# Two column parts of the output projection taken tile by tile with the second norm and the router between them, and the shared gate and up products ahead of the routing counts

## The chip, the cores and the metric

The kernel runs on one core of one Trainium2 chip. The metric is the time of one execution on the device in microseconds (us), the median of several runs. The engines are TensorE (PE), VectorE (DVE), ScalarE (ACT), GpSimd (POOL) and SyncE (SP); SP, ACT and POOL also issue transfers, which the core's 16 DMA engines carry out.

## The reference

One layer of a hybrid decoder step: attention in three groups and a short convolution, one output projection, a second norm, then a mixture of 64 experts with 8 chosen per token. What matters here is the second half:

```python
x = x + g1 * (jnp.concatenate([attn, conv_out], axis=-1) @ w_o)          # 1024 x 1024
h2 = _rmsnorm(x, norm2_g) * (1 + sc2) + sh2
x = x + g2 * _moe(h2, w_router, b_router, ...)

def _moe(h, ...):
    scores = jax.nn.sigmoid(xt @ w_router)                                 # n x 64
    sel = scores + b_router          # top 2 of each group of 8 -> 4 groups -> top 8 experts
    w = w / jnp.sum(w, axis=-1, keepdims=True) * ROUTED_SCALE              # gates
    routed = sum over chosen experts of gate * (silu(x @ w_gate_e) * (x @ w_up_e)) @ w_down_e
    shared = (silu(xt @ w_gate_s) * (xt @ w_up_s)) @ w_down_s              # width 256
    return routed + shared
```

There are 544 tokens (512 of a prompt, 32 of a batch of decode samples), the model width is 1024, an expert's width is 256, and all is in float32.

## The kernel before, in words

The program is written out by hand, engine by engine; each engine runs its own list in the order written and waits on semaphores. Nothing reorders it. The tokens are five tiles in `ORDER`: first the 32 sample tokens (`SAMPLE`, j = 0), then four tiles of 128.

**Output projection.** `w_o` lies in three column parts of 384, 384 and 256 (`WO_W`). The loop runs over parts and inside each over the five tiles, so a unit u is 5 times the part plus the tile. PE computes a unit into bank `pb[u % 2]` (L1356; the sample tile's products, which use a quarter of the columns, at L1166) and may start unit u when the evacuation of unit u - 2 is over (`s_wg`). DVE multiplies the unit by the adaLN gate (L1799) and adds it to x (L1801); for the sample tile it first adds four quarters (L1626, L1628).

**Second norm and router.** When a tile's last part is added, ACT squares and sums its row (L1004), DVE makes mean and epsilon (L1768, `inverse_rms`), ACT takes the root (L1007), DVE inverts it (L1771) and makes the normed row in two instructions (L1784, L1786, `second_norm`); the second one signals `s_h2`. PE turns the row by eight transposes (L1089), ACT copies them to `h2T` (L1019), PE multiplies by the router's weights (L1368), and ACT takes the sigmoid (L1013). In the kernel before DVE does the norms of the first two tiles between the units of the last part, and those of the other three behind the projection; PE's turns and routers stand behind the whole projection.

**Routing.** From all scores DVE selects eight experts per token (L1822 to L1852), which gives the mask `r_mb` (`s_M`). PE counts the tokens of each expert and ranks them (`ranks`, L1396 to L1405), DVE sorts the 64 experts by count (L1873 to L1887, `s_pick`), PE forms the list of expert numbers (`served`, L1412), and DVE writes it to `meta` (L1891, `s_meta`). The gates are a chain of six DVE instructions (L1863 to L1868, `s_G`).

**Shared expert.** Gate and up are computed in two halves f = 0, 1 of the width: a product with `w_gate_s` and one with `w_up_s` for each (PE L1434 and L1437). ACT applies silu (L1031), DVE multiplies (`shared_mul`, L1859). `ranks` stands between the halves, and `served` between gate and up of the second. Then ten units of the down product (`shared_down`, L1453), with `places` (L1420, L1421) behind the first, and two `slots` (L1462) among them, which give the row numbers for the first gathers.

**Weights of the routed experts.** SP first writes the normed rows to DRAM (L591), waits for `s_G` and writes the gates (L594), waits for `s_meta`, reads four expert numbers into registers (L598), and then issues the loads of the first four experts (L602 gate and up, L606 down; 1 MB each, three per expert), the last two of them only after `shared_down`. In the loop of 16 passes, each with four experts, SP reloads a buffer when PE has used it: gate and up of the first two, down of the first two, gate and up of the last two, down of the last two. PE computes gate and up (L1497) and down (L1517); POOL gathers tokens (L766) and adds results to DRAM (L771).

## Time and profile before

| | us |
|---|---|
| median of 3 runs | 1240.82 (1238.19 to 1246.15) |
| the profiled execution, own time | 1241.44 |
| its span in the trace | 1239.6 |
| PE busy | 1088.4 (88%) |
| DVE busy | 436.6 (35%) |
| ACT busy | 210.9 (17%) |
| POOL busy | 257.0 (21%) |
| the chain that ended last, by engine | PE 50%, DMA 36%, DVE 6% |

The trace's times start at the span's start. A timeline row gives start, duration, engine, line of the program, operation, what it writes and reads, the count of instructions merged in it, and in brackets how long the engine had been idle before and what ended that. The chain is followed back from the last instruction: each piece is the work or the wait that the next one was waiting for. PEclk is TensorE's granted clock as a share of its full 2.4 GHz, so 0.5 is 1.2 GHz. The DMA share is the mean busy share of the 16 DMA engines.

### The profile page before, as it was taken

To read this page: it belongs to the slowest core of one execution; us is meant where nothing else is said; L and a number is where in the kernel's file an instruction comes from. 1 tells how busy PE (TensorE), PEld (TensorE's weight loads), DVE (VectorE), ACT (ScalarE), POOL (GpSimd) and SP (SyncE) were. 2 spreads that over 40 slices of the span, in tenths; PEclk is the share of its full clock that TensorE was granted. 3 is DMA by queue.
4 is the path that set the end of the run, shared out by engine and by line. 5 is a ranking of instruction groups with operands and counts; after the bars stand their busy time and mean duration, and the time that the engine had idled before them with its cause. 6 is when DMAs were issued, how large, how long until landed. Compare 5 with 4: busy or idle time off the path is not lost.

```text
span 1239.6 us, 16572 instructions
## 1 busy us (share of the span) xinstructions
PE 1088.4 (88%) x5866; PEld 537.3 (43%) x5866; DVE 436.6 (35%) x985; ACT 210.9 (17%) x455; POOL 257.0 (21%) x276
## 2 busy tenths in 40 slices
PE   6879999997998987989999999989988998899870
PEld 2445445554776565543333333333333333333330
DVE  1324776403456357132323213221322132213225
ACT  4311110002333013021111101110111011111110
POOL 1001223103121200012223122312221223122220
PEclk9989999996999998999999999999999999999995
DMA  9896789936562962197999999999999999999936
GB/s 318 327 345 218 227 287 320 232 127 212 168 190 94 348 239 90 70 411 266 388 384 374 371 381 390 387 370 368 386 388 350 373 376 386 364 358 382 375 88 233
DMA packets 80933, 370.73 MB, mean 299 GB/s; under 512 B 12913, under 2 KB 27358, under 8 KB 52695
## 3 DMA queue, kind: packets, MB, share of 16 engines
q1 hardware_dynamic: 47088, 258.50, 52.3%
q0 software_dynamic: 26176, 79.62, 23.9%
q10 hardware_dynamic: 7636, 32.17, 7.2%
q8 instruction: 21, 0.34, 0.1%
q14 instruction: 12, 0.10, 0.0%
HBM read 342.62 MB, written 66.02 MB: 330 GB/s over the span
## 4 chain that ended last, share of the span: by engine, by line
PE 50%; DMA 36%; DVE 6%; issue 3%; SPq 2%; ACT 1%; POOL 1%; ACTq 0%; DVEq 0%; POOLq 0%
DMA mem<-in_w_up_e 31%; PE pb L1497 14%; PE pb L1201 8%; PE pb L1356 4%; PE pb L1205 3%; PE pb L1517 3%; DMA new_d<-mem 2%; PE pb L1089 2%; PE pb L1116 2%; PE pb L1434 2%; PE pb L1334 2%; PE pb L1288 1%; SPq L602 1%; PE pb L1275 1%; DMA mem<-in_w_ada 1%
## 5 line engine op out<-in xcount | busy, mean ns | idle before, releaser
L1497 PE MATMUL pb<-mem 128*32 128x512 f32 (+2 forms) x1792 | 349.2, 603 | 26.1 <-DMA mem<-in_w_up_e 25.8
L1497 PEld LDWEIGHTS pb<-mem 128*32 128x32 f32 (+2 forms) x1792 | 119.2, 130 | 242.3 <-issue 241.8
L1517 PE MATMUL pb<-mem 128*32 128x512 f32 (+2 forms) x896 | 177.5, 597 | 2.6 <-issue 2.6
L1089 PE MATMUL pb<-mem 128*128 128x128 f32 (+2 forms) x649 | 95.1, 283 | 61.1 <-ACT mem L1046 27.4
L1987 DVE SCALAR_TENSOR_TENSOR mem<-pb,mem 128x256 f32<-128x256 f32 x48 | 32.5, 676 | 319.2 <-ACT mem L1059 250.9
L771 POOL DMA_INDIRECT y_d<-mem x48 | 69.7, 1453 | 302.0 <-DVE mem L1993 160.7
L1201 PE MATMUL pb<-mem 128*128 128x384 f32 x384 | 131.3, 497 | 0.0
L1089 PEld LDWEIGHTS pb<-mem 128*128 128x128 f32 (+2 forms) x649 | 72.6, 146 | 119.4 <-issue 48.4
L1517 PEld LDWEIGHTS pb<-mem 128*32 128x32 f32 (+2 forms) x896 | 57.0, 129 | 97.8 <-issue 97.8
L766 POOL DMA_INDIRECT mem<-h_d,mem x54 | 60.8, 1126 | 179.6 <-issue 135.3
L1201 PEld LDWEIGHTS pb<-mem 128*128 128x128 f32 x384 | 72.5, 193 | 58.2 <-issue 9.6
L1059 ACT ACTIVATE mem<-pb 128x256 f32<-128x256 f32 x48 | 18.4, 383 | 344.2 <-PE pb L1497 344.2
L1993 DVE COPY mem<-pb 128x512 f32<-128x512 f32 x48 | 33.2, 691 | 103.0 <-PE pb L1517 103.0
L1356 PE MATMUL pb<-mem 128*128 128x384 f32 (+1 forms) x192 | 55.9, 452 | 0.0
L771 POOL DMA_INDIRECT z_d<-mem x32 | 45.8, 1432 | 36.7 <-DVE mem L1993 27.8
L1356 PEld LDWEIGHTS pb<-mem 128*128 128x128 f32 x192 | 36.2, 190 | 19.7 <-issue 1.2
L694 POOL DMA_DIRECT2D mem<-in_cache_k_w x24 | 12.8, 535 | 153.7 <-DVE mem L1620 96.7
L1930 DVE TENSOR_TENSOR mem<-mem 128x320 bf16<-128x320 f32 (+3 forms) x90 | 43.8, 551 | 2.0 <-DMA y_d<-mem 2.0
L1958 DVE COPY mem<-pb 128x512 f32<-128x512 f32 x51 | 35.3, 692 | 23.5 <-PE pb L1089 23.2
L1205 PE MATMUL pb<-mem 128*128 128x512 f32 x96 | 42.7, 597 | 0.0
L1068 ACT ACTIVATE mem<-pb 128x512 f32<-128x512 f32 x48 | 28.6, 595 | 76.9 <-PE pb L1517 76.9
L1046 ACT ACTIVATE mem<-pb 128x512 f32<-128x512 f32 x51 | 30.5, 597 | 48.2 <-PE pb L1089 48.2
(261 smaller groups left out, 984.1 us busy)
## 6 DMA issues: line engine op xcount, KB each, us to landing
mem<-in_w_gate_e SPq DMA_DIRECT2D x64, 1024.0 KB, 15.4
mem<-in_w_up_e SPq DMA_DIRECT2D x64, 1024.0 KB, 24.2
mem<-in_w_down_e SPq DMA_DIRECT2D x64, 1024.0 KB, 22.8
mem<-in_w_ada SPq DMA_DIRECT2D x24, 1024.0 KB, 10.0
mem<-in_w_in SPq DMA_DIRECT2D x8, 1536.0 KB, 14.1
mem<-new_d POOLq DMA_DIRECT2D x16, 512.0 KB, 6.9
out<-in_cache_k_w ACTq DMA_DIRECT2D x8, 1020.0 KB, 14.9
out<-in_cache_v_w ACTq DMA_DIRECT2D x8, 1020.0 KB, 20.3
```

The lines of the kernel that those rows point to most:

```text
L766: eng.indirect_dma_start(out=xg[t][:], out_offset=None, in_=h2_d, in_offset=bass.IndirectOffsetOnAxis(ap=ix[:, t:t + 1], axis=0), bounds_c ...
L771: eng.indirect_dma_start(out=to, out_offset=bass.IndirectOffsetOnAxis(ap=ixs[0:hi - lo, col:col + 1], axis=0), in_=yo[t][lo:hi, :], in_off ...
L1089: return eng.transpose(dst, src, ident[0:parts, 0:parts])
L1201: mm = eng.matmul(pb[z % 2][0:nt(tt), 0:PJ_W], lhsT=hT[:, k, tok(tt)], rhs=w[:, k, :], start=(k == 0), stop=(k == KD - 1))
L1205: eng.matmul(pb[z % 2][:, :], lhsT=w[:, k, P * j:P * (j + 1)], rhs=hT[:, k, 0:SEQ], start=(k == 0), stop=(k == KD - 1))
L1356: mm = eng.matmul(pb[u % 2][0:nt(tt), 0:WO_W[o]], lhsT=catT[:, k, tok(tt)], rhs=w[:, k, :], start=(k == 0), stop=(k == KD - 1))
L1497: mm = eng.matmul(pb[t % 2][lo:hi, :].rearrange("p (q f) -> p q f", q=2), lhsT=xT[t][:, k, lo:hi], rhs=wgu[c][:, :, k, :], start=(k == 0), ...
L1517: mm = eng.matmul(pb[2 + half][lo:hi, :], lhsT=he[t][:, f, lo:hi], rhs=wdn[c][:, f, 512 * half:512 * half + 512], start=(f == 0), stop=(f ...
L1930: last = eng.tensor_tensor(oneh[:, :, lo:lo + n], pos[:, :, at_].to_broadcast([P, TILES, n]), const("place")[:, p0:p0 + n].unsqueeze(1).to ...
L1958: eng.tensor_copy(xT[t][:, 4:8, :], pb[5][:, :].rearrange("p (k n) -> p k n", k=4)).then_inc(s_xd, 1)
L1987: eng.scalar_tensor_tensor(out=hh[t].rearrange("p (k f) -> p f k", k=2), in0=pairs(pb[t % 2][:, FE:2 * FE]), scalar=gcol[t], in1=pairs(sge ...
L1993: eng.tensor_copy(yo[t][:, 512:D], pb[3][:, :]).then_inc(s_yd, 1)
```

## The change

The projection's parts 1 and 2 are taken tile by tile (`WO_UNITS`): part 0 over all tiles as before, then for each tile its unit of part 1 and its unit of part 2. The norm of tile j - 1 is split on DVE around the second unit of tile j, and PE's turn of tile j - 1 and router of tile j - 2 follow PE's two units of tile j (`NORMED`). Four small DVE instructions that prepare routing tables move from the end of the projection to between part 0 and part 1. ACT's work takes the same order. Both halves of the shared gate and up stand ahead of `ranks`; the rest of the routing follows, then `places`, and then `shared_down` without a break but for `slots`, two units earlier than before. DVE's `shared_mul(0)` moves ahead of the mask and the gates' chain behind `shared_mul(1)`. `w_up_s` gets a buffer of its own (slot 10) and is loaded behind `w_gate_s`; SP issues the load of `w_down_s` ahead of the last normed row.

```diff
+WO_UNITS = [(0, j) for j in range(TILES)] + [(o, j) for j in range(TILES) for o in (1, 2)]
 def wo_done(u):
-    return u + 1 + 3 * (u // 5 + 1)
+    return u + 1 + 3 * sum(ORDER[j] == SAMPLE for _, j in WO_UNITS[:u + 1])
+NORMED = ((), (0,), (1,), (2,), (3, 4))
...
-    slots += [0, 1, 2, 0, 1, 2]
+    slots += [0, 1, 2, 0, 10, 2]
...
         ring += [at(m, ADA_W) for m in (m_mod, m_mod + ADA_W, m_qk + NVEC * VL, m_qk + NVEC * VL + ADA_W, m_cv,
-                                        m_vr + 512, m_att)]
+                                        m_vr + 512, m_att, m_mod + HROW)]
...
+                kind, i = items[n]
+                if kind == "sup":
+                    eng.wait_ge(s_add, 16)
+                    eng.wait_ge(s_fold, len(WIDE))
...
-                        eng.wait_ge(s_wo, wo_done(5 * i0 + 4))
+                        eng.wait_ge(s_wo, wo_done(WO_UNITS.index((i0, TILES - 1))))
...
+            last = ring_uses("sdown", 0)
+            for n in range(last):
+                ring_load(n)
             for j, tt in enumerate(ORDER):
+                if j == TILES - 1:
+                    ring_load(last)
                 eng.wait_ge(s_h2, j + 1)
                 eng.dma_start(h2_d[tok(tt), 0:D], h2_row[j % 2][0:nt(tt), :]).then_inc(s_h2w[j % 2], 16)
             eng.wait_ge(s_G, 1)
...
             eng.wait_ge(s_scb, 16 * ZW)
+            eng.wait_ge(s_su, 4)
             load_dn(1, first[1])
-            eng.wait_ge(s_su, 4)
...
+            for j in range(TILES):
+                squares(j)
+                for i in NORMED[j]:
+                    turned(i)
+                    if i:
+                        if i == 1:
+                            eng.wait_ge(s_rz, 1)
+                        sigmoid(i - 1)
             sigmoid(TILES - 1)
             for f in range(2):
-                if f:
-                    eng.wait_ge(s_route, 2)
-                    eng.activation(rT[:, 0:512], pb[0][0:NE, :], ACT.Copy)
-                    eng.activation(rT[:, 512:TILES * P], pb[1][0:NE, 0:P], ACT.Copy).then_inc(s_rT, 1)
                 eng.wait_ge(s_su, 2 * f + 1)
                 eng.activation(sg[:, f, 0:SEQ], pb[4 * f][:, :], ACT.Silu)
                 eng.activation(sg[:, f, SEQ:NTOK], pb[4 * f + 2][:, 0:NS], ACT.Silu).then_inc(s_sg, 1)
+            eng.wait_ge(s_route, 2)
+            eng.activation(rT[:, 0:512], pb[0][0:NE, :], ACT.Copy)
+            eng.activation(rT[:, 512:TILES * P], pb[1][0:NE, 0:P], ACT.Copy).then_inc(s_rT, 1)
...
+            for u in range(TILES):
+                project(u)
+            for j in range(TILES):
+                project(TILES + 2 * j)
+                project(TILES + 2 * j + 1)
+                for i in NORMED[j]:
+                    second_turn(i)
+                    if i:
+                        router(i - 1)
             router(TILES - 1)
...
             for f in range(2):
                 if f:
-                    ranks()
                     eng.wait_ge(s_sc, TILES)
                 for q, n in ((0, n_g), (1, n_u)):
-                    if f and q:
-                        eng.wait_ge(s_pick, 1)
-                        served(0, NE)
                     w = ring[slots_of[n]][:, 0:KD * FE].rearrange("p (k n) -> p k n", k=KD)
                     for k in range(KD):
                         eng.matmul(pb[4 * f + q][:, :], lhsT=w[:, k, P * f:P * (f + 1)], rhs=h2T[:, k, 0:SEQ],
                         mm = eng.matmul(pb[4 * f + q + 2][:, 0:NS], lhsT=w[:, k, P * f:P * (f + 1)],
                                         rhs=h2T[:, k, SEQ:NTOK], start=(k == 0), stop=(k == KD - 1))
                     mm.then_inc(s_su, 1)
+            ranks()
+            eng.wait_ge(s_pick, 1)
+            served(0, NE)
             eng.wait_ge(s_pick, 2)
             eng.matmul(pb[2][0:NE, 0:1], lhsT=upper[0:NE, 0:NE], rhs=e_units, start=True, stop=True)
             eng.matmul(pb[2][0:1, 1:2], lhsT=ones[0:NE, 0:1], rhs=e_units, start=True, stop=True
                        ).then_inc(s_route, 1)
             ring_in(n_d)
             wd = ring[slots_of[n_d]][:, 0:2 * D].rearrange("p (k n) -> p k n", k=2)
-            eng.wait_ge(s_hs, 2)
             def shared_down(u):
...
+            eng.wait_ge(s_pick, 3)
+            served(NE, P)
+            eng.wait_ge(s_sg, 2)
+            places()
+            eng.wait_ge(s_hs, 2)
             for u in range(10):
                 shared_down(u)
-                if u == 0:
-                    eng.wait_ge(s_pick, 3)
-                    served(NE, P)
-                    places()
-                if u == 5:
+                if u == 3:
                     slots(0)
-                if u == 8:
+                if u == 6:
                     eng.wait_ge(s_ix, 1)
                     slots(1)
             eng.wait_ge(s_ysh, 10)
...
+            def gated_sum(u):
...
+                eng.wait_ge(s_wo, wo_done(u))
...
+                    whole = part[:, 0:w]
+                eng.tensor_tensor(wt[u % 2][0:n, 0:w], whole, m2[s][0][0:n, c0:c0 + w], ALU.mult).then_inc(s_wg, 1)
+                eng.wait_ge(s_wg, u + 1)
+                eng.tensor_tensor(x_t[0:n, tt, c0:c0 + w], x_t[0:n, tt, c0:c0 + w], wt[u % 2][0:n, 0:w], ALU.add
+                                  ).then_inc(s_x1, 1)
+            for u in range(TILES):
+                gated_sum(u)
             eng.wait_ge(s_vout, 16 * (DIL * G + 1))
             link(eng.memset(r_mb, 0.0))
...
-            for j in range(2, TILES):
-                inverse_rms(j)
-            for j in range(2, TILES):
-                second_norm(j)
+            for j in range(TILES):
+                gated_sum(TILES + 2 * j)
+                if j:
+                    inverse_rms(j - 1)
+                gated_sum(TILES + 2 * j + 1)
+                if j:
+                    second_norm(j - 1)
+            inverse_rms(TILES - 1)
+            second_norm(TILES - 1)
             link(eng.tensor_copy(slotb[:, 0:15], const("slot")[:, 0:15]))
...
-            link(eng.reciprocal(r_den, r_den))
-            link(eng.tensor_scalar(r_den, r_den, 2.5, None, ALU.mult))
-            eng.tensor_tensor(r3(r_g), r3(r_g), r_den.unsqueeze(2).to_broadcast([P, TILES, NE]), ALU.mult
-                              ).then_inc(s_G, 1)
+            eng.tensor_tensor(r_mb[:, 0:SAMPLE * NE], r_ma[:, 0:SAMPLE * NE], r_mr[:, 0:SAMPLE * NE], ALU.not_equal
+                              ).then_inc(s_M, 1)
+            eng.tensor_tensor(r_mb[0:NS, SAMPLE * NE:RW], r_ma[0:NS, SAMPLE * NE:RW], r_mr[0:NS, SAMPLE * NE:RW],
+                              ALU.not_equal).then_inc(s_M, 1)
...
             link(eng.tensor_reduce(e_iters[0:1, :], e_small[0:1, :], AX, ALU.add))
             link(eng.tensor_scalar(meta[0:1, P:P + 1], e_iters[0:1, :], float(QUART), None, ALU.add))
             shared_mul(1)
+            link(eng.tensor_tensor(r_g, r_sc, r_mb, ALU.mult))
+            link(eng.tensor_reduce(r_den, r3(r_g), AX, ALU.add))
+            link(eng.tensor_scalar(r_den, r_den, 1e-30, None, ALU.max))
+            link(eng.reciprocal(r_den, r_den))
+            link(eng.tensor_scalar(r_den, r_den, 2.5, None, ALU.mult))
+            eng.tensor_tensor(r3(r_g), r3(r_g), r_den.unsqueeze(2).to_broadcast([P, TILES, NE]), ALU.mult
+                              ).then_inc(s_G, 1)
```

Place 1, PE in parts 1 and 2. Before, behind part 2 (L1356 is the projection, L1089 the turn of a normed row, L1368 the router; 128x256 is a unit of part 2):

```order
L1356 MATMUL pb<-mem 128x256 [waits s_wg]
L1356 MATMUL pb<-mem 128x256 x7
L1356 MATMUL pb<-mem 128x256 [waits s_wg]
L1356 MATMUL pb<-mem 128x256 x7
L1089 MATMUL pb<-mem 128x32 [waits s_h2,s_wr]
L1089 MATMUL pb<-mem 128x32 x7
L1089 MATMUL pb<-mem 128x128 [waits s_h2T,s_h2]
L1089 MATMUL pb<-mem 128x128 x3
L1089 MATMUL pb<-mem 128x128 [waits s_h2T]
L1089 MATMUL pb<-mem 128x128 x3
L1368 MATMUL pb<-mem 32x64 [waits s_h2T]
L1368 MATMUL pb<-mem 32x64 x7
```

Of the change, the units of tile 1, the turn of tile 0, the units of tile 2 and the turn of tile 1 (L1382 is the projection, L1114 the turn):

```order
L1382 MATMUL pb<-mem 128x384 [waits s_wg,s_ring1]
L1382 MATMUL pb<-mem 128x384 x7
L1382 MATMUL pb<-mem 128x256 [waits s_wg,s_ring2]
L1382 MATMUL pb<-mem 128x256 x7
L1114 MATMUL pb<-mem 128x32 [waits s_h2]
L1114 MATMUL pb<-mem 128x32 x7
L1382 MATMUL pb<-mem 128x384 [waits s_wg,s_ring1]
L1382 MATMUL pb<-mem 128x384 x7
L1382 MATMUL pb<-mem 128x256 [waits s_wg,s_ring2]
L1382 MATMUL pb<-mem 128x256 x7
L1114 MATMUL pb<-mem 128x128 [waits s_h2T,s_h2]
L1114 MATMUL pb<-mem 128x128 x3
```

The turn of the tile before, with its wait for `s_h2`, now stands directly behind a tile's unit of part 2, and the next tile's unit of part 1 stands behind the turn.

DVE at the same place of the change (L1834 and L1836 evacuate a unit, L1802 and L1805 are `inverse_rms`, L1818 and L1820 `second_norm`, the last of which signals `s_h2`; tile 1, norm of tile 0):

```order
L1834 TENSOR_TENSOR mem<-pb,mem 128x384 [waits s_wo]
L1836 TENSOR_TENSOR mem<-mem 128x384 [waits s_wg]
L1802 TENSOR_SCALAR mem<-mem 32x1 [waits s_ss2]
L1805 RECIPROCAL mem<-mem 32x1 [waits s_sd2]
L1834 TENSOR_TENSOR mem<-pb,mem 128x256 [waits s_wo,s_m2,s_link]
L1836 TENSOR_TENSOR mem<-mem 128x256 [waits s_wg]
L1818 SCALAR_TENSOR_TENSOR mem<-mem 32x1024
L1820 TENSOR_TENSOR mem<-mem 32x1024 [waits s_link]
```

The norm of tile 0, which stood among the evacuations of part 2, now follows the evacuation of tile 1's unit of part 2, which waits for PE by `s_wo`.

Place 2, DVE behind the tokens' selection. Before (L1859 and L1860 are `shared_mul(0)`, L1863 to L1868 the gates' chain, then the sorting of experts):

```order
L1859 TENSOR_TENSOR mem<-pb,mem 128x512 [waits s_sg,s_su,s_M]
L1860 TENSOR_TENSOR mem<-pb,mem 128x32
L1863 TENSOR_TENSOR mem<-mem 128x320
L1864 TENSOR_REDUCE mem<-mem 128x5 [waits s_link]
L1865 TENSOR_SCALAR mem<-mem 128x5 [waits s_link]
L1866 RECIPROCAL mem<-mem 128x5 [waits s_link]
L1867 TENSOR_SCALAR mem<-mem 128x5 [waits s_link]
L1868 TENSOR_TENSOR mem<-mem 128x320 [waits s_link]
L1873 SCALAR_TENSOR_TENSOR mem<-pb,mem 64x64 [waits s_route]
L1875 SCALAR_TENSOR_TENSOR mem<-pb,mem 64x1
```

Of the change, ten rows behind the expert numbers' copy to `meta` (L1940 is the last of the iterations' count, L1893 and L1894 are `shared_mul(1)`, L1942 to L1947 the gates' chain):

```order
L1940 TENSOR_SCALAR mem<-mem 1x1 [waits s_link]
L1893 TENSOR_TENSOR mem<-pb,mem 128x512 [waits s_sg,s_su,s_link]
L1894 TENSOR_TENSOR mem<-pb,mem 128x32
L1942 TENSOR_TENSOR mem<-mem 128x320
L1943 TENSOR_REDUCE mem<-mem 128x5 [waits s_link]
L1944 TENSOR_SCALAR mem<-mem 128x5 [waits s_link]
L1945 RECIPROCAL mem<-mem 128x5 [waits s_link]
L1946 TENSOR_SCALAR mem<-mem 128x5 [waits s_link]
L1947 TENSOR_TENSOR mem<-mem 128x320 [waits s_link]
```

The chain of the gates moved from ahead of the sorting to behind `shared_mul(1)`, so that `s_G` now comes later than `s_meta`.

SP at the same place of the change (L612 writes the gates, L616 reads the expert numbers into registers; the first load, L620, stands behind four such readings):

```order
L612 DMA h_d<-mem 128x64 [waits s_G]
L612 DMA h_d<-mem 128x64 x3
L612 DMA h_d<-mem 32x64
L616 TENSOR_LOAD mem [waits s_meta]
L616 ISA x2
```

SP's order here did not move: the gates' rows with their wait for `s_G` stand ahead of the wait for `s_meta` and of the first load.

Place 3, PE at the shared gate and up. Before (L1434, L1437 the products, L1396 to L1405 `ranks`, L1412 `served`):

```order
L1434 MATMUL pb<-mem 128x512 x8
L1437 MATMUL pb<-mem 128x32 x8
L1396 MATMUL pb<-mem 64x64 [waits s_hs,s_M]
L1396 MATMUL pb<-mem 64x64 x4
L1399 MATMUL pb<-mem 64x1 x5
L1405 MATMUL pb<-mem 64x128 x15
L1434 MATMUL pb<-mem 128x512 [waits s_sc]
L1434 MATMUL pb<-mem 128x512 x7
L1437 MATMUL pb<-mem 128x32 x8
L1412 MATMUL pb<-mem 1x64 [waits s_pick]
L1434 MATMUL pb<-mem 128x512 x8
```

Of the change (L1465, L1468 the products, L1431 to L1440 `ranks`, L1447 `served`):

```order
L1465 MATMUL pb<-mem 128x512 [waits s_sc]
L1465 MATMUL pb<-mem 128x512 x7
L1468 MATMUL pb<-mem 128x32 x8
L1465 MATMUL pb<-mem 128x512 x8
L1468 MATMUL pb<-mem 128x32 x8
L1431 MATMUL pb<-mem 64x64 [waits s_hs,s_M]
L1431 MATMUL pb<-mem 64x64 x4
L1434 MATMUL pb<-mem 64x1 x5
L1440 MATMUL pb<-mem 64x128 x15
L1447 MATMUL pb<-mem 1x64 [waits s_pick]
```

`ranks` stood behind the first half; it now stands behind both, and `served` follows it at once.

## Rows read from the trace of the kernel before

**Rows 1.** Chain that ended last, in order of time: start, duration, piece of work.

```profile
486.79 6.92 PE pb L1434 x16
493.71 1.71 PE pb L1437 x16
...
558.49 10.68 PE pb L1497 x48
...
596.75 10.63 PE pb L1497 x48
...
665.59 29.83 DMA mem<-in_w_up_e
...
695.65 7.10 PE pb L1497 x32
...
736.87 8.80 PE pb L1497 x32
```

**Rows 2.** Windows: stretch and length; PEclk, DMA share, GB/s.

```profile
520.00:560.00 40.00, 0.96 0.96 392
560.00:576.00 16.00, 1.00 0.50 161
576.00:665.00 89.00, 1.00 1.03 378
665.00:1148.00 483.00, 0.99 1.01 376
```

**Rows 3.** Timeline of SP's issues: start, duration, row.

```profile
507.07 2.22 SPq L594 DMA_DIRECT2D h_d<-mem  x5
520.32 0.36 SPq L602 DMA_DIRECT2D mem<-in_w_gate_e  x1
```

**Rows 4.** Timeline of PE, projection to shared down: start, duration, row, idle ahead.

```profile
424.43 20.91 PE L1356 MATMUL pb<-mem 128*128 128x384 f32 x64
...
446.27 14.08 PE L1356 MATMUL pb<-mem 128*128 128x256 f32 x64
...
470.06 1.94 PE L1089 MATMUL pb<-mem 128*128 128x128 f32 x8 [9.11 <-ACT mem L1019]
...
482.18 1.10 PE L1089 MATMUL pb<-mem 128*128 128x128 f32 x8 [1.23 <-DVE mem L1786]
...
528.83 2.98 PE L1453 MATMUL pb<-mem 128*32 128x512 f32 x4 [2.74 <-DVE mem L1860]
```

**Rows 5.** Timeline of DVE, evacuations and norms in the projection.

```profile
424.64 0.55 DVE L1626 COPY mem<-pb 32x384 f32<-32x384 f32 x1 [0.38 <-PE pb L1166]
...
426.99 0.55 DVE L1799 TENSOR_TENSOR mem<-mem 32x384 f32<-32x384 f32 x1
...
454.87 2.07 DVE L1784 SCALAR_TENSOR_TENSOR mem<-mem 32x1024 f32<-32x1024 f32 x1
...
458.91 0.41 DVE L1799 TENSOR_TENSOR mem<-pb,mem 128x256 f32<-128x256 f32 x1
```

**Rows 6.** Timeline of PE in the input projection.

```profile
155.91 0.37 PE L1089 MATMUL pb<-mem 32*128 32x32 f32 x3 [1.90 <-DVE mem L1665]
...
157.20 7.12 PE L1201 MATMUL pb<-mem 128*128 128x384 f32 x16
```

**Rows 7.** Window of PE: stretch, length, busy; PEclk, DMA share, GB/s.

```profile
464.00:475.00 11.00, 4.74 (x29) 0.53 0.41 150
```

**Rows 8.** Timeline of DVE, gates' chain to the expert numbers.

```profile
504.87 0.48 DVE L1863 TENSOR_TENSOR mem<-mem 128x320 f32<-128x320 f32 x1
...
506.96 0.21 DVE L1873 SCALAR_TENSOR_TENSOR mem<-pb,mem 64x64 f32<-64x64 f32 x1
...
508.84 0.15 DVE L1887 TENSOR_REDUCE mem<-mem 64x1 f32<-64x8 f32 x1
517.04 0.22 DVE L1891 CAST mem<-pb 1x64 int32<-1x64 f32 x1 [8.05 <-PE pb L1412]
526.13 0.23 DVE L1898 TENSOR_SCALAR mem<-mem,pb 1x16 f32<-1x16 f32 x1 [8.87 <-PE pb L1442]
```

## What the change is expected to do

> **What bounds the kernel now.** I read the chain of waits first, since it says which engine the end hangs on at each time. It runs on PE from the shared gate product at 486.8 to the first pass of the expert loop at 558.5, and on in passes of 38.2 us (558.49 to 596.75); from 665.6 it goes over to the landing of expert weights, and PE's product for the last two experts then starts every 41.2 us (695.65 to 736.87) [rows 1]. So one sees PE first and transfers later. The chain does not say how much room the transfers had before 665. The windows do: from 576 to 1148 the DMA engines are full (share 1.03 and 1.01, 378 and 376 GB/s); from 520 to 560 they are as good as full too (0.96, with the start in it); only from 560 to 576 is the share 0.50, that is 16 x 0.50 = 8.0 us of idle transfer time [rows 2]. SP issues the first expert load at 520.3 [rows 3]. The amount of data from there on is fixed. So from the first load to the end of the loop the kernel has 8.0 us of slack in its transfers, and a first load that comes later by more than that moves the end, unless PE holds it back more. Two quantities are needed: how much later (or earlier) the first load is issued, and how much PE's loop start moves. The time of the first load is made up of S, the start of the shared gate product (486.8 before), and what lies between S and the load.
>
> **The projection, before S.** Before, the projection ends at 446.27 + 14.08 = 460.3, PE then sits idle 9.1 us for DVE's norms, and S follows at 486.8, 26.5 us after the projection's end [rows 1, 4]. The change takes routers and turns under the projection, but a wait goes with them. On PE the turn of tile j - 1 stands directly behind tile j's unit of part 2; on DVE the norm of tile j - 1 stands behind the evacuation of that same unit. The norm therefore cannot start until PE has finished the unit, and PE has nothing to do but wait for it. The wait is an evacuation, two instructions of about 0.42 or 0.9 us with gaps, and a norm, 454.87 to 458.91 or 4.1 us [rows 5], with 0.1 for signals: 5.1 us. Queued behind the waiting turn are the router and the next tile's two units; ACT's copies and SP's row writes come after it in any case. It happens for tiles 1, 2 and 3 within the projection: 3 x 5.1 = 15.3 us.
>
> The sample tile costs too. DVE now has four small instructions ahead of its evacuation in part 1. The nearest row, one over 320 columns, takes 0.48 [rows 8], so they are between nothing and 1.9 us; two of them are on half as many columns and less, and I take 1.1. Before, DVE began the evacuation at 424.6 after 0.4 us of idle and its multiply ended at 426.99 + 0.55 = 427.5 [rows 5]; it is now 0.7 later, 428.3. PE needs only 1.1 us more for the sample tile's unit of part 2 from 424.4, to 425.5, and its next unit wants that bank: 2.8 us of idle PE.
>
> Turns and routers moved ahead: a turn is 1.1 us, and two routers take the 3.5 us from 483.28 to 486.79 [rows 1, 4]. Turns of tiles 0 to 2 (0.7 + 1.1 + 1.1) and routers of 0 and 1 (3.5) add 6.5 us to the projection's end: 460.3 + 2.8 + 15.3 + 6.5 = 484.9. Behind it stand an evacuation 0.9, norm of tile 3 4.1, `inverse_rms` 0.6 and norm of tile 4 4.1, under which PE's turn and router of earlier tiles are hidden, and then the same 4.6 us as before from the last turn to S (482.18 to 486.79): 14.3 us. S at full clock is 499.2, which is 12.4 us later than before. The 26.5 us behind the projection do shrink to 14.3; the waits inside cost more than that gives. The extra changes of ACT's function tables (four more) stand in ACT's waiting times; without that cover each lies ahead of a root or a sigmoid. I take nothing for them.
>
> **The clock.** What PE did before the clock fell: the 9.1 us of idle ahead of 470.06 [rows 4] are followed by the stretch 464 to 475 with a granted clock of 0.53, the lower level, 1.2 GHz [rows 7], and there a turn takes 1.94 where it takes 1.10 at full clock. After only 1.90 us idle and a short turn, a unit of 128x384 takes 7.12 us [rows 6], where the projection takes 20.91 / 4 = 5.2 [rows 4]: 1.9 us lost. The turn at 482.18, behind 1.23 us of idle, shows no such loss. The waits of the change are 2.8 and three of 5.1 before S, each ahead of units of that kind, so the bounds are 0 (none falls) and 4 x 1.9 = 7.6 (all fall); they lie nearer to the rows that lose, and I take 7.6. The fourth wait of 5.1 is behind the projection, where PE waits for the last norm anyway, and costs nothing. S comes to 506.8, 20.0 us later.
>
> The Trainium skill, page "TensorE: Matmul & The Clock Gate", section "HAM oscillation — how this bites in real kernels", describes just this pattern: a wait that returns with every tile drops the clock anew each time, so that every tile starts at the half rate and the cost is paid per tile. By that rule the term is 7.6; by the row of 482.18 alone, where a short idle cost nothing, it would be 0. The two losing rows of this trace agree with the rule.
>
> **From S to the first load.** A gate or up product is 6.92 + 1.71 = 8.63 us [rows 1]. Four of them now precede `ranks`, 34.5 us. From the start of `ranks`: 0.5 us until DVE has the counts, its sorting 2.0 (506.96 to 508.99), 0.5 for PE's two small products, 2.6 for the next DVE stretch with `shared_mul(1)` (526.13 to 528.7, where PE resumes [rows 4]), and then the gates' chain 2.1 (504.87 to 506.96): `s_G` at 7.7 [rows 8]. `s_meta` is ready earlier, but SP's queue has the gates' rows first: 2.2 us of issuing [rows 3], and then the reading of four expert numbers, 520.32 - 517.26 = 3.1 us [rows 3, 8]. This reading was not behind `s_G` before; the gates' rows had been written at 507 to 509, 8 us ahead of `s_meta`. The first load is at S + 34.5 + 7.7 + 2.2 + 3.1 = S + 47.5, against S + 33.5 before: 14.0 us more. Loads start 20.0 + 14.0 = 34.0 us later, at 554.3.
>
> **The sum.** Less the 8.0 us of slack the end is 26.0 us later, if the idle of 560 to 576 goes away fully. It does if the second pass's loads are issued before the first twelve have landed: those kept the engines full for some 40 us before, so now until about 595; PE's loop start moves to about 574 (next), and it frees the first buffers 14.8 us later, at 589. PE itself moves less: from S to the loop was 71.7 us [rows 1], and of that the 2.7 us of idle ahead of `shared_down` [rows 4] and a clock loss behind it of 1.9 or so go away, as both halves are then done: 20.0 - 4.6 = 15.4 us later. So transfers decide. Own time of the profiled execution 1241.4 + 26.0 = 1267.4; it stands 0.6 above the median of 1240.8, so 1267. The earlier `slots`, the buffer for `w_up_s` (loaded behind `w_gate_s`, used 60 us later) and the later issue of `w_down_s` move neither quantity.
>
> **Rivals.**
> - PE decides: the late loads are caught up in the passes, which PE takes at 38.2 and transfers at 41.2. For it speaks that the chain is on PE until 665; against it the full share from 576 on. The end moves with PE, 15.4 us: 1256.
> - The clock stays up in all waits: 26.0 - 7.6 = 18.4 later, 1259. Against it rows 6 and 7. Together with the first rival: 20.0 - 7.6 - 4.6 = 7.8, or 1249, within 1% of before.
> - The norms are hidden, as the change's words say: PE's turn finds its row ready. The 15.3 and three of the four clock losses (5.7) go: 26.0 - 21.0 = 5.0, or 1246. Against it the order of both engines, in which nothing can move.
> - Faster or no slower, by one mechanism: the transfers' pass gets shorter, because loads meet gathers and scatters at another phase. While weights alone move, the rate would allow it: PE's own pass is 38.2. Over 15 passes the loss of 26.0 is made up when a pass falls by 1.7 us, to 39.5; at 38.4 the kernel would be at 1241.4 + 26 - 42, 1225. Against it: 378 GB/s in 576 to 665 and 376 after it, though the phase differs.
>
> **Chances and range.** The forecast has 0.75, PE decides 0.07, full clock 0.07, both together 0.04, hidden norms 0.03, shorter passes 0.04. The likeliest's own range is 1259 (no clock loss) to 1275 (each clock loss 2.5 us, and SP's reading or the norms' signals 1 us each dearer). The range to all but 2 in 10 is 1252 to 1275. A measurement can tell about 1% from no change, 12 us. Faster by over 1%: 0.03; within 1%, 1228 to 1253: 0.07; slower 0.90.
>
> **What the profile would show.** Four idle stretches of PE of about 5.1 us ahead of the turns in the projection, put down to DVE's second norm instruction, and one of 2.8 after the sample tile; PEclk at half behind them; S near 507; the gates' rows issued near 549 and the first expert load near 554, behind `s_meta` by over 5 us; no window of share 0.5 between the first load and 600; the chain on transfers from the second pass on instead of the fourth. I am wrong if PE turns without waiting, if the share falls below 1 after the first load, or if passes differ from 41.2 us.

## The result, and the profile after

The changed kernel takes 1263.65 us (median of 4 executions, 1262.48 to 1268.09) against 1239.72 for the kernel before on the same chip (4 executions): ratio 1.0181, 95% interval 1.0137 to 1.0225. It is slower, by 23.9 us; forecast were 26.

In the fourteen traces the output projection begins at 394.95 to 400.74 us, ahead of the first changed instruction that matters, while kernels with the same order from there on agree within 1 us in the distances behind it. So I compare distances: from the projection's start (call it P) to S (start of the shared gate product), from S to L (first pass of the expert loop), from L to the end of the span. P is this row, of the kernel before and then of the changed kernel (start, duration, row, idle ahead):

```profile
400.74 1.50 PE L1166 MATMUL pb<-mem 128*32 128x384 f32 x16 [0.81 <-issue]
```

```profile
394.95 1.50 PE L1191 MATMUL pb<-mem 128*32 128x384 f32 x16 [0.81 <-issue]
```

The chain of waits of the changed kernel, which answers to [rows 1]:

```profile
502.89 6.92 PE pb L1465 x16
509.81 1.71 PE pb L1468 x16
...
556.19 0.37 PE pb L1495 x15
...
561.13 17.05 DMA mem<-h_d,mem
...
578.31 1.94 PE pb L1114 x8
580.25 11.20 PE pb L1531 x48
...
619.04 10.63 PE pb L1531 x48
...
679.25 7.04 PE pb L1531 x32
...
687.87 29.66 DMA mem<-in_w_up_e
```

| | before | after | change | forecast |
|---|---|---|---|---|
| P to S | 486.79 - 400.74 = 86.1 | 502.89 - 394.95 = 107.9 | +21.9 | +20.0 |
| S to L | 558.49 - 486.79 = 71.7 | 580.25 - 502.89 = 77.4 | +5.7 | -4.6 |
| L to the end | 1239.6 - 558.49 = 681.1 | 1260.6 - 580.25 = 680.4 | -0.8 | +10.6 |
| P to the end | 838.9 | 865.7 | +26.8 | +26.0 |

(The medians differ by 23.9: that these two traces give 26.8, and their bare spans 21.0, is the scatter of P and of single executions.) The first row and the sum are about as forecast; the second and third are both wrong, and cancel. In the chain one sees what is new: ahead of the loop PE hangs on a gather of 17.05 us, the third of three (before it was the first one, and 7.39 us, see below; of the three, the slowest took 8.2 us before), and behind the loop's start the chain stays on PE for 106 us (580.25 to 686.3), nearly as before (107, 558.49 to 665.6), then goes over to transfers. It does not go over at the second pass.

The timeline of PE in the projection, where [rows 4] showed one wait of 9.11 us:

```profile
422.46 8.85 PE L1382 MATMUL pb<-mem 128*128 128x384 f32 x32 [2.88 <-DVE mem L1834]
436.37 1.05 PE L1114 MATMUL pb<-mem 32*128 32x32 f32 x8 [5.06 <-DVE mem L1820]
437.36 11.02 PE L1382 MATMUL pb<-mem 128*128 128x384 f32 x32
453.81 1.97 PE L1114 MATMUL pb<-mem 128*128 128x128 f32 x8 [5.43 <-DVE mem L1820]
455.70 1.91 PE L1404 MATMUL pb<-mem 128*32 128x64 f32 x16
457.55 9.47 PE L1382 MATMUL pb<-mem 128*128 128x384 f32 x32
472.08 1.68 PE L1114 MATMUL pb<-mem 128*128 128x128 f32 x8 [5.06 <-DVE mem L1820]
473.56 3.52 PE L1404 MATMUL pb<-mem 128*128 128x64 f32 x16
476.86 10.02 PE L1382 MATMUL pb<-mem 128*128 128x384 f32 x32
491.94 1.97 PE L1114 MATMUL pb<-mem 128*128 128x128 f32 x8 [5.05 <-DVE mem L1820]
```

L1820 is the norm's second instruction on DVE. The waits are those of the forecast: 2.8 (2.88) and four of 5.1 (5.06, 5.43, 5.06, 5.05). Behind each of the four the clock is down (granted 0.50, 0.50, 0.55 and 0.50 in 437 to 441, 454 to 458, 472 to 476 and 492 to 497): a unit of 8.85 us takes 11.02, 9.47, 10.02, a turn of 1.09 takes up to 1.97. Behind the wait of 2.88 it is not (1.00 in 422 to 431).

The windows, which answer to [rows 2]: stretch, length, busy times, then PEclk, DMA share and GB/s at the end of the row.

```profile
422.00:503.00 81.00, 59.95 (x249) 46.00 (x250) 32.48 (x45) 20.20 (x36) 0.56 (x1) 0.81 0.40 155
572.00:580.00 8.00, 5.51 (x24) 4.77 (x25) 1.84 (x5) 1.75 (x3) 0.00 (x0) 0.50 1.02 423
580.00:1148.00 568.00, 519.40 (x2990) 207.49 (x2989) 148.86 (x403) 80.87 (x169) 149.22 (x116) 0.99 1.01 376
592.00:600.00 8.00, 8.00 (x50) 2.68 (x46) 1.53 (x5) 1.50 (x4) 0.00 (x0) 1.00 0.75 299
```

From 572 to 580, where PE turns the gathered rows at half clock, the transfers are full. The gap behind the first loads is still there, at 592 to 600: 8 x 0.25 = 2.0 us idle, of the 8.0 before. SP's timeline answers to [rows 3]:

```profile
545.19 2.22 SPq L612 DMA_DIRECT2D h_d<-mem  x5
550.53 0.36 SPq L620 DMA_DIRECT2D mem<-in_w_gate_e  x1
551.56 0.33 SPq L620 DMA_DIRECT2D mem<-in_w_gate_e  x1
...
553.92 0.33 SPq L620 DMA_DIRECT2D mem<-in_w_gate_e  x1
```

The first load stands at S + 47.6 (550.53 - 502.89); forecast was S + 47.5. Last, ACT's timeline, where it evacuates the shared rows (L1064) and sends them to memory (`y_d`):

```profile
559.41 1.31 ACT L1064 ACTIVATE mem<-pb 128x512 f32<-128x512 f32 x2 [2.58 <-DMA y_d<-mem]
...
565.95 1.09 ACT L1064 ACTIVATE mem<-pb 128x512 f32<-128x512 f32 x2 [5.23 <-DMA y_d<-mem]
...
570.78 1.08 ACT L1064 ACTIVATE mem<-pb 128x512 f32<-128x512 f32 x2 [3.74 <-DMA y_d<-mem]
```

ACT sits 11.6 us idle for the writes of earlier rows (8.2 before), since there are two row buffers, and PE's turn at the end of this waits 4.50 us for ACT. Rows' writes and gathers are both issued while expert weights are in flight: the third gather is issued 10.6 us behind the first load (561.13 - 550.53), where it was 28.4 us before (548.75 - 520.32). The same place in the chain of the kernel before:

```profile
543.82 0.37 PE pb L1462 x15
...
545.82 7.39 DMA mem<-h_d,mem
```

### The profile page after: what moved, and what is told of

It is laid out like the page before. It is cut to its first block, busy times and chain, and to the rows that moved or that the text cites. A ratio compares the mean times of both kernels' runs of the same rounds, so it can differ in the third digit from the quotient of the medians.

```text
span 1260.6 us, 16592 instructions
## 1 busy us (share of the span) xinstructions
PE 1098.2 (87%) x5866; PEld 545.0 (43%) x5866; DVE 435.8 (35%) x985; ACT 216.2 (17%) x459; POOL 256.7 (20%) x276
## 4 chain that ended last, share of the span: by engine, by line
PE 54%; DMA 33%; DVE 6%; issue 2%; ACT 1%; SPq 1%; POOL 1%; ACTq 0%; DVEq 0%; POOLq 0%
DMA mem<-in_w_up_e 28%; PE pb L1531 15%; PE pb L1226 8%; PE pb L1382 5%; PE pb L1551 4%; PE pb L1230 3%; PE pb L1114 3%; PE pb L1465 2%; DMA new_d<-mem 2%; PE pb L1141 2%; PE pb L1359 2%; DMA mem<-h_d,mem 1%; PE pb L1313 1%; SPq L620 1%; PE pb L1300 1%
## 5 line engine op out<-in xcount | busy, mean ns | idle before, releaser
L1114 PE MATMUL pb<-mem 128*128 128x128 f32 (+2 forms) x649 | 99.4, 292 | 75.4 <-ACT mem L1071 25.7
L1114 PEld LDWEIGHTS pb<-mem 128*128 128x128 f32 (+2 forms) x649 | 76.5, 152 | 133.5 <-issue 42.1
L1084 ACT ACTIVATE mem<-pb 128x256 f32<-128x256 f32 x48 | 18.4, 383 | 344.8 <-PE pb L1531 344.8
L1382 PE MATMUL pb<-mem 128*128 128x384 f32 (+1 forms) x192 | 60.3, 475 | 2.9 <-DVE mem L1834 2.9
L789 POOL DMA_INDIRECT z_d<-mem x32 | 45.9, 1433 | 36.4 <-DVE mem L2032 27.6
L1382 PEld LDWEIGHTS pb<-mem 128*128 128x128 f32 x192 | 38.2, 202 | 24.2 <-issue 7.7
```

The source lines that it names most:

```text
L789: eng.indirect_dma_start(out=to, out_offset=bass.IndirectOffsetOnAxis(ap=ixs[0:hi - lo, col:col + 1], axis=0), in_=yo[t][lo:hi, :], in_off ...
L1114: return eng.transpose(dst, src, ident[0:parts, 0:parts])
L1382: mm = eng.matmul(pb[u % 2][0:nt(tt), 0:WO_W[o]], lhsT=catT[:, k, tok(tt)], rhs=w[:, k, :], start=(k == 0), stop=(k == KD - 1))
```

## The experiments

Two theories. **A:** the end follows L at a fixed 681 us, and L is late by the projection and by small transfers that stand behind weights. **B:** the end follows the first expert load, less the slack. B is the prediction's rule without its clause "unless PE holds it back more"; with the clause the rule is the later of the two, and it gives A wherever the loads still have room. The first four experiments split the change and its two halves.

**Only the projection.** The change's projection and turns, the routing of before: `shared_gate_up` of the second half behind the counts, the gates' chain ahead of sorting.

> The projection of the change (tile by tile, own buffer for w_up_s) with the routing order of before. Shared gate starts 18 to 19 us later than before, the first expert load the same 18 to 19 us later. Theory A (PE's loop start decides): the way from there to the loop is 71.7 us as before, so the loop and the end are 18 to 19 us later, near 1258 to 1259. Theory B (transfers decide, 8.0 us of slack): 18.5 - 8 = 10.5 us later, 1250 to 1251.

**Only the routing.** The reverse: the projection of before, and the change's order from S on.

> The projection of the kernel before (all units, then the turns and routers as before) with the change's order of the routing. Both theories put the start of the shared gate product at 486-488 us, the first expert load at 527-530 (8-10 later than before, by the gates' chain that now stands behind sorting) and the idle share of the DMA engines ahead of 600 us larger than before. Theory A (the end follows the start of PE's expert loop): from S to the loop 76-78 us, as in the changed kernel, so a loop start at 563-565 and a time of 1245-1247 (4-6 over before). Theory B (the part from the gate product on costs only what the first load's delay leaves over the slack in the transfers): 8-10 us fit in the 8 us of slack, 1241-1243.

**Turn one tile later,** on PE, all else as changed:

```diff
             for j in range(TILES):
                 project(TILES + 2 * j)
+                if j >= 2:
+                    second_turn(j - 2)
+                    if j > 2:
+                        router(j - 3)
                 project(TILES + 2 * j + 1)
-                for i in NORMED[j]:
-                    second_turn(i)
-                    if i:
-                        router(i - 1)
+            second_turn(3)
+            router(2)
+            second_turn(4)
+            router(3)
             router(TILES - 1)
```

> The change, but PE's turn of tile j - 1 and the router behind it stand behind the first unit of tile j + 1 instead of directly behind the second unit of tile j. Both theories: the waits of 5.1 us inside the projection go (15.3 us) and three losses of clock with them (5 to 6 us); shared gate starts near 483 instead of 503. The end falls by about 20 us to 1243 to 1245, still a few us above before (1240), because the routing order of the change is kept. If it stays above 1255, the waits on the norm were not what cost.

**Turn one tile later, routing of before.**

> The projection tile by tile with the turn one unit later (as in e2_turn_later) and the routing order of before. Shared gate starts 3 to 5 us earlier than before, and the rest is as before: theory A (the end follows PE's loop start) gives 1235 to 1237 against 1240 before; theory B gives the same or, where transfers decide, the same 3 to 5 us, since loads and loop move together.

The medians, the ratios to the kernel before on the same chip with intervals (its median is 1239.72 to 1242.25 by chip), and the distances, all read on PE's timeline (which puts S and L up to 0.2 us off the chain of waits above):

| projection, routing | median, us | ratio | P to S | S to L | L to end |
|---|---|---|---|---|---|
| before, before | 1239.72 | 1 | 85.9 | 71.9 | 681.1 |
| before, changed | 1246.82 | 1.0037 [1.0014, 1.0061] | 85.9 | 78.4 | 680.7 |
| changed, before | 1262.6 | 1.016 [1.0097, 1.0223] | 107.8 | 73.6 | 681.2 |
| changed, changed | 1263.65 | 1.0181 [1.0137, 1.0225] | 107.8 | 77.3 | 680.5 |
| later, changed | 1245.72 | 1.0022 [0.9995, 1.0049] | 84.0 | 77.3 | 681.2 |
| later, before | 1236.62 | 0.995 [0.9925, 0.9976] | 84.1 | 70.7 | 680.1 |

In these traces the first load stands 29.5 to 41.5 us ahead of L, and the last column does not move with it. In the run with the projection alone the first load was only 18.3 us later than before (538.57 against 520.32 [rows 3]), the loop 21.6: the end came 21.7 later in the span (1261.3 against 1239.6). That is A; by B it would have been 18.3 - 8.0 = 10.3, and by the prediction's rule with its clause 21.6, like A. A's own figure, 1258 to 1259, was missed by 4 us, as the loop moved 21.6 and not 18 to 19. The place of the turn is all of the projection's cost: 107.8 becomes 84.0, below the 85.9 of before. In the trace with the later turn only the last of the four waits of 5.1 us is left (5.06 us at 469.19), beside the 2.88. And the routing costs time with two of the projections: S to L is 78.4 or 77.3 where the old order has 71.9 or 70.7. With the changed projection it is 77.3 against 73.6, and the ratios, 1.0181 and 1.016, do not tell the two apart; part of the 73.6 is a lower clock ahead of the gathers (20 instructions of `shared_down` in 10.65 us instead of 8.97).

**Gates' chain first.** The changed kernel with the gates' block on DVE (L1942 to L1947) ahead of sorting again, so that only the first load moves.

> The changed kernel with the gates' chain on DVE (five operations and the product) put back ahead of the sorting. Both theories: the gates' rows go out and the first expert load is issued 4-6 us earlier (545-546 instead of 550.5). Theory A (the end follows the loop start, which waits for the gathers and the shared rows' writes): the loop start does not come earlier, 579-583, since the ranks, and with them the gathers, come some 3-5 us later and stand behind the loads; time 1262-1266. Theory B (the first load's place decides, as the prediction had it): 5 us less, 1257-1259.

1267.56 us, 1.0197 [1.0153, 1.0241]. SP's and then PE's timeline:

```profile
548.37 0.36 SPq L620 DMA_DIRECT2D mem<-in_w_gate_e  x1
```

```profile
507.82 7.09 PE L1465 MATMUL pb<-mem 128*128 128x512 f32 x16
...
585.10 11.42 PE L1531 MATMUL pb<-mem 128*128 128x512 f32 x48
```

The first load is at S + 40.6 instead of S + 47.8 on this timeline, 7.2 us earlier; L is at S + 77.3 and the end at L + 680.7, both as in the changed kernel. B is out: 7.2 us of the first load's place are worth nothing here. The prediction's rule with its clause is not, since an earlier load cannot bring the end ahead of PE's.

**Gathers ahead of the third expert's loads.** In SP's program:

```diff
             load_dn(1, first[1])
+            for t in range(ET):
+                eng.wait_ge(s_ga[t], 16)
             load_gu(2, first[2])
```

> The change, but SP waits for the first three gathers to have landed before it issues the loads of the third and fourth expert. Theory A (the end follows PE's loop start, and in the change that start is late because the first gathers, 17.1 us to landing, and the shared expert's row writes stand behind 10 MB of expert weights): the gathers land some 8 us earlier, near 568 to 570 us, the loop starts 5 to 8 us earlier than the change's 580.3, and the kernel takes 1256 to 1259 us. Theory B (the end follows the amount of transfer from the first load on, as predicted): the transfers of the third and fourth expert start later, so the kernel takes the change's 1264 us or up to 6 us more.

1269.47, 1.0195 [1.0143, 1.0248]. L at S + 76.6: a miss. ACT's writes held PE as before (4.56 us), and from L to the end it was 684.4, 3.9 us longer. The third gather took 15.8 us.

**A third row buffer,** so that ACT need not wait for the writes of tiles 0 and 1: `y_row[j % 3]` with a semaphore of its own, in memory where SP loads the fourth expert's gate and up only later.

> The changed kernel with a third buffer for the rows of the shared expert, so that ACT's evacuation of tiles 2 and 3 no longer waits for the write of tile 0 and 1 to memory (2.58 + 5.23 + 3.74 = 11.6 us of waits in the trace of after, and PE's 4.50 us ahead of the turns of the first expert behind it). If that wait is what sets the loop's start: PE's 4.5 us go, less what the third gather (landing at 578.2) then holds: loop start 575.5-578 instead of 580, time 1259-1262. If the gathers decide alone: 579-580 and 1263.

1267.07, 1.0198 [1.0155, 1.0242]; L at S + 77.2, as the expectation's second case has it, but slower than its 1263. PE's timeline ahead of the loop shows what took the wait's place:

```profile
572.55 1.07 PE L1115 MATMUL pb<-mem 128*128 128x128 f32 x8 [1.00 <-DMA mem<-h_d,mem]
577.35 1.94 PE L1115 MATMUL pb<-mem 128*128 128x128 f32 x8 [3.73 <-DMA mem<-h_d,mem]
582.38 1.94 PE L1115 MATMUL pb<-mem 128*128 128x128 f32 x8 [3.09 <-DMA mem<-h_d,mem]
```

No turn waits for ACT any more (4.50 us in the changed kernel), but the three turns wait 7.8 us for the three gathers, issued at 562.33, 563.96 and 565.27.

**Both together.**

> The changed kernel with both causes taken away at once: the third buffer for the shared rows, and SP issues the loads of the third expert only when the three gathers of the first have landed. One of the two alone left the start of the expert loop at S + 76.6 and S + 77.2 us (S: start of the shared gate product), since the other took its place. If the rows' writes and the gathers behind the bulk loads are the whole of what the part from S to the loop is longer than forecast, the loop now starts at S + 72 to 74, 3-5 us earlier than in the changed kernel, and the time is 1259-1262, if the loads held back do not come back later (in the run with the gathers ahead alone, 3.9 us were lost from the loop's start to the end, 684.4 instead of 680.5). If it is something else (the ranks, POOL's three issues), S + 77 again.

1269.59, 1.0223 [1.018, 1.0266], a miss: L at S + 76.6, the third gather still 16.29 us, from L to the end 684.9. So holding the third expert's loads does not relieve the gathers: 6 MB of the first two experts' weights are issued ahead of them in any case (10 MB in the changed kernel).

**Gathers ahead of all but the first 2 MB.** The same three waits of SP, but behind `load_gu(0, ...)`, in the kernel with two row buffers.

> The changed kernel, with SP holding all expert loads but the first expert's gate and up (2 of the 6 MB that stand ahead of the gathers in the changed kernel) until the three gathers have landed. If the gathers take 17 us because these megabytes stand before them: 7-9 us each instead of 10-17, third landing at S + 66-68 instead of S + 75.4, the rows' writes faster too, and the loop starts at S + 68-70 instead of 77.3. The price is what the held loads cost later: they start some 13 us later than in the changed kernel. If the end follows the loop's start alone, 8 us earlier, 1255-1257; if the transfers decide once they are this late, the loop's gain is given back: 1262-1268. If the gathers stay at 17 us, the loads are not their cause.

1271.0, 1.0235 [1.0195, 1.0275]. The chain of waits of this run:

```profile
566.26 6.91 DMA mem<-h_d,mem
...
578.21 30.42 DMA mem<-in_w_up_e
...
608.86 9.67 PE pb L1533 x32
```

The gather takes 6.91 us instead of 17.05, ACT waits at most 2.30 us for a write instead of 5.23, and L is at S + 70.7 (578.55 - 507.86), 6.6 us earlier. The cause of the late loop is thereby shown: weights ahead of the small transfers. The chain also shows the price. The weights held back land at 608.6 and PE waits 8.27 us in its first pass; from L to the end it is 690.5, 10 us more, and the time is above the 1262 to 1268 expected. So the slack of the loads does end.

**Where it ends.** The transfers of all fourteen traces say it. SP's first reload of a used buffer comes 14.8 to 16.1 us behind L. Windows from about L + 4 to L + 20 of the changed kernel, then gates' chain first, gathers ahead of the third expert, gathers ahead of all but 2 MB:

```profile
584.00:600.00 16.00, 16.00 (x94) 5.35 (x96) 4.45 (x11) 2.02 (x5) 4.86 (x7) 1.00 0.88 360
589.00:605.00 16.00, 16.00 (x94) 5.42 (x96) 4.46 (x11) 2.02 (x5) 4.90 (x7) 1.00 0.55 188
588.80:604.80 16.00, 16.00 (x94) 5.42 (x96) 4.09 (x11) 2.02 (x5) 4.78 (x7) 1.00 1.01 403
582.50:598.50 16.00, 16.00 (x100) 5.36 (x102) 3.96 (x11) 2.02 (x5) 4.37 (x7) 1.00 1.02 418
```

The changed kernel still has 16 x 0.12 = 1.9 us of idle transfers there, gates' chain first has 7.2 (its loads are 7.2 us earlier), the kernel before 6.9. In the eleven traces with an end at L + 680.1 to 681.2 the idle time is 1.4 to 8.3 us; in the three with a later end (684.4, 684.9, 690.5) there is none. From L + 20 on all fourteen move 376 or 377 GB/s. So the transfers do set the pace of the rest, and the idle share is the room of the first loads, but counted from L: while some of it is left, the stream that decides begins with the reloads, which PE releases, and the end follows L. Up to L + 20 the eleven have moved 18.8 to 19.3 MB (in the changed kernel 49.5 us at 384 GB/s), the run with all but 2 MB held 15.2: the missing 3.8 MB are 10.1 us at 377 GB/s, and the end is 10.0 us later. For the other two, 18.3 and 18.1 MB, this gives about 2 us of the 3.9 and 4.4.

**Matmuls in the waits.** Work that nothing reads is added ahead of the turns:

```diff
+                if j <= 3:
+                    for k in range(5 if j else 3):
+                        eng.matmul(pb[6][:, :], lhsT=catT[:, k % KD, tok(0)], rhs=catT[:, k % KD, 0:SEQ],
+                                   start=(k == 0), stop=(k == (4 if j else 2)))
                 for i in NORMED[j]:
                     second_turn(i)
```

> The changed kernel with matmuls of 512 columns that nothing reads, put ahead of the turns in the first four tiles of the output projection (3, then 5 in each of three), where PE waits for the norm: added work, for the clock's sake. If the clock losses behind the waits are a cost of the change (prediction: 4 of 1.9 us; the trace of after: three units of 11.02, 9.47 and 10.02 us where 8.85 is the full-clock one), the granted clock stays at 1.0 through the projection, the three units take 8.85, the shared gate product starts at 497-499 instead of 502.7, and the end comes 4-6 us earlier than the changed kernel's: 1257-1260. If the losses come from something else than the idle time, or the added matmuls take longer than the waits they fill (5 x 0.22 = 1.1 of 5.1 us each at full clock, so there is room), the time stays at 1263 or rises.

1264.34, 1.0168 [1.0123, 1.0213], a miss of the 1257 to 1260 expected: the time cannot be told from the changed kernel's. PE's timeline:

```profile
436.28 4.45 PE L1415 MATMUL pb<-mem 128*128 128x512 f32 x10
441.52 0.69 PE L1114 MATMUL pb<-mem 32*128 32x32 f32 x8 [0.79 <-DVE mem L1824]
442.14 8.88 PE L1382 MATMUL pb<-mem 128*128 128x384 f32 x32
...
489.02 1.97 PE L1114 MATMUL pb<-mem 128*128 128x128 f32 x8 [5.06 <-DVE mem L1824]
490.78 3.51 PE L1404 MATMUL pb<-mem 128*128 128x64 f32 x16
494.08 1.92 PE L1114 MATMUL pb<-mem 128*128 128x128 f32 x8
495.79 6.93 PE L1404 MATMUL pb<-mem 128*128 128x64 f32 x32
502.51 8.31 PE L1469 MATMUL pb<-mem 128*128 128x512 f32 x16
```

Five such matmuls take 4.45 us, four times my figure, and still fit in the wait. The three units take 8.88, 8.88 and 8.83 instead of 11.02, 9.47 and 10.02: it is PE's idle time that lost the clock. P to S falls from 107.8 to 102.4, as expected. But the unfilled wait at 489 now costs more (a router of 6.93 instead of 4.17, a first product of 8.31 instead of 7.08), and S to L grows by 1.7 to 79.0. From P to the end 3.3 us are left of 5.4 (862.4 against 865.7).

**Two versions on top of the best one,** the later turn with the old routing. The first has the third row buffer and DVE's fills of the routing tables behind the sample tile's two parts; the second only the buffer.

> A version meant to be faster than both: each tile's norm, turn and router one tile later under the projection, the routing in the order of the kernel before, a third buffer for the shared rows, and DVE's fills of the routing tables moved behind the sample tile's parts, so that PE does not wait 2.88 us for them. Against the version without the last two (1236.62, ratio 0.995): the 2.88 us ahead of tile 0 go, and the 8.18 us write that held ACT before the loop goes off the chain, which the third gather (landing at 550) lets through for 0.7 us. Expected 1232-1235, ratio 0.992; if the freed time in the projection only makes a norm late, 1236.

> The version with each tile's turn one tile later and the routing of the kernel before (1236.62, ratio 0.995), with nothing but the third buffer for the shared rows added. In its trace an 8.18 us write held ACT right before the expert loop (2.21 us of wait of PE); the third gather lands some 0.7-1 us before that turn. Expected the same within 1 us: 1235.5-1237, ratio 0.994-0.995. If the version with both additions (1238.72, 0.9976) was slower because of this buffer and not of the moved fills, 1238-1239.

1238.72, 0.9976 [0.9953, 0.9999], and 1238.02, 0.9978 [0.9955, 1.0001]: neither is better than the 0.995 they start from. The first missed its 1232 to 1235; the second is at the 1238 to 1239 named for the case that the buffer is what costs, but its interval overlaps that of 0.995. PE's wait behind the sample tile fell only from 2.88 to 2.32 us in the first. S to L was 74.1 and 72.6 instead of 70.7: the first gather still took 8.66 us in the second, and PE waited for gathers (3.00 us) where it had waited for ACT (2.21). Part of the 74.1 is a lower clock behind a wait of 2.74 us ahead of `shared_down` (20 instructions in 10.81 us, where the version without these edits, and the one with the buffer only, have 8.97 behind a wait of the same 2.74). Best remains the later turn with the routing of before: 1236.62 us, half a per cent faster than before.

## Why the prediction was right in size and wrong in a step

- **The waits of the projection: right.** Place, number, releaser and length are those of the forecast, and with the turn one tile later all but the last of the four are gone, and P to S is 84.0 instead of 107.8.
- **The clock: right in sum, not in its parts.** Forecast were four losses of 1.9. The trace has none behind 2.88 us; behind the other three the units lose 4.0 us together (2.2, 0.6, 1.2), and turns and routers at half clock 4.2 (1.97 for 1.09, 3.52 for 1.90, and 1.05 for the sample tile's 0.69). The step "the fourth wait costs nothing" was wrong: behind it turns and routers run at half clock, and from the last turn to S it is 5.7 us (497.22 to 502.89) instead of 4.6, and the slow turn and router ahead of the last turn hold it back by another 0.4. That is 1.5 of the 1.9 by which the term was short. Ahead of it, losses of 8.2 against 7.6, waits of 2.88 + 5.06 + 5.43 + 5.06 = 18.4 against 18.1 and units 0.5 longer in sum are nearly balanced by turns and routers moved ahead, which at full clock are 5.3 and not 6.5 us (the sample tile's router takes 1.0, not half of 3.5). The rule of the Trainium skill, page "TensorE: Matmul & The Clock Gate", section "HAM oscillation — how this bites in real kernels", that each such wait drops the clock anew, agrees with four of five waits here. It speaks of longer waits than the one of 2.88 us, which lost nothing, so the 7.6 that the prediction worked out by it counts one loss too many.
- **S to the first load: right** to 0.1 us (47.6 against 47.5).
- **S to L: the mis-sized term.** The step was "PE itself moves less ... 20.0 - 4.6 = 15.4". Up to the counts it held nearly: the last small product ahead of the gathers is at S + 53.3 (556.19) against S + 57.0 before (543.82 in the trace of before), 3.7 earlier. What I left out is that the three gathers and the row writes are then issued while the first ten MB of weights are in flight (the third gather 10.6 us behind the first load, before 28.4): the forecast moved SP's loads towards POOL's gathers and ACT's writes and counted only SP's queue. The three gathers took 6.4 to 8.2 us before and 10.2 to 17.0 now. The term was +5.7 instead of -4.6, off by 10.3.
- **"So transfers decide": it did not come to that, because of the step before.** The prediction's rule takes the later of two: the loads' delay less the room of 8.0 us, and the delay of the loop's start. Counted from P, the loads came 36.0 us later (155.6 against 119.6; forecast 34.0), which leaves 28.0, and the loop's start came 27.6 later, not 15.4. The first load stood 29.5 us ahead of L instead of 38.2, the gap behind the first loads shrank from 8.0 to 2.0 us, and the end followed L. By the rule the gap should have just closed, so such a reckoning is good to about 2 us. That is the mechanism of the first rival, "PE decides" (given 0.07), at another size: 21.9 + 5.7 - 0.8 = 26.8. The rule itself, idle share as room for the loads counted from L, fits the fourteen traces, where the end moves away from L only in the three without a gap; what no run tests is the forecast's own case, loads 34 us and the loop 15 us later.
- **The hit is in part luck.** The loads' path was right to 2 us, but it did not set the end. The loop's start did, and it slipped, for a cause the forecast had not, by about as much as that path: 10.3 us in the step from S to L stood in the place of the 10.6 us by which the forecast let the transfers be later than PE.
- **Against the signs named at the end:** waits, PEclk, S and first load as said (S near 507 by the clock of before: 400.74 + 107.9 = 508.7; the load at 556.3). "No window of share 0.5 between the first load and 600" held (0.75 in 592 to 600), but "I am wrong if the share falls below 1 after the first load" came true by the same window, and "the chain on transfers from the second pass on" was wrong: it goes over 106 us behind L, as before.

Open: why the two kernels with the third expert's loads held pay about 4 us, where the missing megabytes give 2. Also open is what all of the pricier S to L of the last two versions rests on; each has one trace.

## What to carry to other kernels

When a step is to be hidden behind the next tile's work, count on both engines what its operand waits for: a turn placed directly behind the unit whose evacuation goes ahead of its norm waits each time, and one unit later it does not. Where bulk loads are issued, list every small transfer on any queue that is issued while they are in flight and that an engine waits for: it can pay for the megabytes ahead of it (17 us instead of 7 here). And the idle share of the DMA engines behind a prefetch is its slack only against the start of the loop that uses it: the later loads are bound by buffers and move with the engine that frees them. So forecast both delays with equal care, look in the trace whether the gap is still there, and find the invariant distance over two or three traces before trusting either.

## What was not expected of the hardware

- The third gather of the first expert took 17.05, 17.44, 17.16, 17.14 and 16.97 us in five kernels where it was issued 10.5 to 11.3 us behind the first of ten megabytes of loads, 17.05 in one where it was 17.8 us behind, 15.8 and 16.29 behind six, and 6.91 behind two; with 28.4 us or more between them the slowest of the three took 9.7 at most. So it does not grow in step with the megabytes. POOL issues the gathers and SP the loads: another issuing engine did not put the gathers ahead. That agrees with the Trainium skill, page "DMA: Bandwidth & Descriptors", section "Issuing engines are not separate DMA queues": transfers interleave on the same 16 DMA engines whichever engine started them.
- The clock did not fall behind 2.88 us of idle in the projection, fell behind every idle stretch of 5.05 us or more there, and behind 2.74 us ahead of `shared_down` it was lower in two traces (10.65 and 10.81 us for what takes 8.97) and not in three.
- Where the clock had been held up by added matmuls, the next unfilled wait cost more: two stretches of the same instructions took 6.93 and 8.31 us instead of 4.17 and 7.08.
